# A decoder layer with 32 experts: expert outputs added into one array by accumulating scatters, and two-part matmuls in the narrow visits

## The chip, the cores and the metric

The kernel runs on one core of a Trainium2 chip. The core has TensorE (PE, with its weight loads shown apart as PEld), VectorE (DVE), ScalarE (ACT), GpSimd (POOL) and SyncE (SP, which here only issues DMAs). The metric is the device time of the whole program in microseconds (us).

## The reference

A layer norm, a combined input projection, a causal pooling mixer beside sparse attention (each query attends to the 256 keys that an indexer selects), an output projection, a residual with a layer norm (its result is called h1 here), and then a mixture of experts with a last residual and layer norm. What the change touches is the mixture of experts and what follows it:

```python
top_logit, top_e = lax.top_k(logits, TOP_K)          # 4 of 32 experts for each of 2048 tokens
gates = jax.nn.softmax(top_logit, axis=-1)
xs = xf[tok]                                         # 8192 rows of 1024, sorted by expert
hu = lax.ragged_dot(xs, w_gate_up, group_sizes) + b_gate_up[e_sorted]   # 1024 -> 2048
gate = jnp.minimum(hu[:, :D_FF], 7.0);  up = jnp.clip(hu[:, D_FF:], -7.0, 7.0)
act = (up + 1.0) * gate * jax.nn.sigmoid(1.702 * gate)
y = lax.ragged_dot(act, w_down, group_sizes) + b_down[e_sorted]         # 1024 -> 1024
out = jnp.zeros_like(xf).at[tok].add(y * g_sorted[:, None])
h = layer_norm(2 ** 0.25 * h + out, ln2_g, ln2_b)
```

All arrays are float32. With the reference's own inputs the experts get, sorted, 356 338 337 329 309 300 300 300 297 285 277 272 269 268 267 261 258 252 249 246 239 235 227 227 209 207 202 200 193 185 167 131 rows.

## The kernel before

Five stages follow each other, each a block with a barrier at its end: projection (to about 640 us of the span), attention with router (to 1840), a short placing stage (to 1854), the experts (to 4387) and the combination (to 4529).

**The experts stage** goes over "visits". A visit is one expert with up to 384 of its rows; here there are 32, widest first. An expert's row count is rounded up to a class of `WIDTHS` (L64: 384, 368, ... 240 in steps of 16), and PE runs one unrolled loop per class (`visit`, L2059; `loop`, L2083). Every engine goes through the visits in its own fixed program order:

- SP streams 12 MB of weights in six chunks of 2 MB through three buffers `w_raw` (`chunk`, L1878). Chunks 0 to 3 hold gate and up weights, 4 and 5 the down weights. It also stores the third row tile of the visit before (`store_third`, L1900), in 12 small DMAs.
- ACT rounds each chunk to `w_hi` (`high`, L2180), DVE computes the rest `w_lo = w_raw - w_hi` (`low`, L2102). The rows `x` are split the same way into `x_hi` and `x_lo`. Each product is then three fast-format matmuls: hi*hi, hi*lo, lo*hi (`passes`, L1995).
- Up part (`up_chunk`, L2007): for each of 8 blocks j of 128 hidden columns, 24 matmuls make the gate sum and 24 the up sum, into the two halves of PSUM pair `gu[j % 2]`. So 8 * 48 = 384 matmuls per visit, each as wide as the class. DVE adds bias, clips, and multiplies (`out_of_psum`, `activate`, L2114 to L2132), ACT does the sigmoid and rounds to `a_hi`, POOL makes `a_lo` and a copy `a_rest` (L1972). DVE and ACT work at 384 columns in every class.
- Down part (L2065): six tiles n of 128 rows x 512 columns in `yp[n % 2]`: n = 0, 1, 2 for the first half of the columns, 3, 4, 5 for the second. The third row tile (n = 2, 5) is a packed short form below 321 rows and nothing at 256 rows or fewer. Between them PE turns the rows of the next visit (`e_tr`). ACT copies each tile to `y_rows` (three buffers, `store`, L2204) and writes the first two row tiles of each half into `y_dram`, an array with one row for each (visit, place).
- POOL fetches the list of the next visit's tokens and gathers their rows of h1 (`gather`, L1953), at the head of the body, once the current visit's `x` has been turned.

**The combination stage** (L2257) gathers for each of 16 tiles of 128 tokens the 4 rows of `y_dram` that belong to each token (64 gathers of 128 rows of 4 KB, L2327), sums them with the gates by matmul (L2369) on top of a matmul for the gated `b_down` (L2362), and DVE and POOL do residual and layer norm (L2397 to L2415). Before that, positions of all picks are worked out on DVE and sent through DRAM to get them in pick order (`pos_list`, `gate_list`). `y_dram` is cleared for the spare visits by 12 DMAs in the projection stage (L615).

**The lists.** In the attention stage's routing DVE works out each token's place in its experts' lists (`weigh`, L1305), and POOL scatters the token numbers there (L1186), one DMA per pick.

## Time and profile before

| | us |
|---|---|
| median of 3 runs | 4528.32 (4526.23 to 4531.88) |
| span of the profiled execution | 4529.3 |
| experts stage, first up matmul to the end of the last visit | 1880.5 to 4381 |
| combination stage | 4387 to 4529.3 |

The page gives the profiled execution no other time of its own than its span, which is 1.0 us above the median of the runs. A busy share is the time in which an engine had at least one instruction running; PE's matmuls overlap in the records (each is shown longer than the distance to the next one), so the pace is read from the length of a stretch divided by its matmuls. Whole stages can be bound by different engines, so shares are read per stretch.

### The profile page before, as it was taken

Reading aid. Unit: us, or ns where it says so; the run is one execution under the profiler, and the core shown is the slowest. Engines: PE = TensorE matmul, PEld = TensorE weight load, DVE = VectorE, ACT = ScalarE, POOL = GpSimd, SP = SyncE. Lnnn points to the kernel's source line nnn. Section 1 sums busy time; section 2 is a strip of 40 time slices with the busy share of each in tenths; the row PEclk is TensorE's granted clock in tenths of the full one; section 3 lists DMA queues with packets and bytes.
Section 4 is the critical chain, followed back from the end, with each engine's and each line's share of the span. In section 5 each row is a group of like instructions: output and inputs, shape, how many; then the busy total and the mean of one; then the engine's idle time right before and its main releaser. Section 6 shows DMA issues by size and latency. Waiting matters only on the chain. (4 is left out here: it accounts for less than half of the span.)

```text
span 4529.3 us, 70549 instructions
## 1 busy us (share of the span) xinstructions
PE 4289.9 (95%) x24356; PEld 3153.5 (70%) x24356; DVE 3076.1 (68%) x4861; ACT 1817.6 (40%) x2677; POOL 1010.1 (22%) x1152
## 2 busy tenths in 40 slices
PE   8999988999999998699999999999999999999987
PEld 4444434444444454599989889899999999999961
DVE  2587867878888873555556556666676777777768
ACT  1222223443434433233434444444445555555530
POOL 1111101221111122211112212222222222222235
PEclk9999989999999999799999999999999999999986
DMA  6443330120110010544555456474657667667668
GB/s 194 126 122 92 87 101 16 30 27 21 18 23 16 14 27 19 148 158 148 174 168 190 155 183 220 162 250 161 237 197 239 208 230 241 219 234 237 212 214 362
DMA packets 534140, 665.72 MB, mean 147 GB/s; under 512 B 64416, under 2 KB 402592, under 8 KB 533952
## 3 DMA queue, kind: packets, MB, share of 16 engines
q1 hardware_dynamic: 419664, 501.02, 34.7%
q10 hardware_dynamic: 87744, 77.15, 5.4%
q0 software_dynamic: 26576, 85.56, 5.0%
q8 instruction: 87, 1.43, 0.1%
q14 instruction: 69, 0.57, 0.0%
HBM read 543.61 MB, written 120.03 MB: 147 GB/s over the span
## 5 line engine op out<-in xcount | busy, mean ns | idle before, releaser
L2000 PE MATMUL gu<-x_hi,w_hi 128*128 128x240 f32 (+8 forms) x4096 | 1196.5, 292 | 4.1 <-issue 4.1
L2003 PE MATMUL gu<-x_lo,w_hi 128*128 128x240 f32 (+8 forms) x4096 | 1195.5, 292 | 0.5 <-issue 0.5
L2004 PE MATMUL gu<-x_hi,w_lo 128*128 128x240 f32 (+8 forms) x4096 | 1194.1, 292 | 0.0
L2106 DVE TENSOR_TENSOR w_lo<-w_raw,w_hi 128x2048 fp32r<-128x2048 f32 x386 | 874.6, 2287 | 414.1 <-ACT w_hi L2190 386.2
L2190 ACT ACTIVATE w_hi<-w_raw 128x2048 fp32r<-128x2048 f32 x386 | 726.8, 1908 | 207.4 <-PE gu L2004 132.0
L2000 PEld LDWEIGHTS gu<-x_hi,w_hi 128*128 128x128 f32 x4096 | 774.7, 189 | 4.5 <-issue 4.3
L2003 PEld LDWEIGHTS gu<-x_lo,w_hi 128*128 128x128 f32 x4096 | 773.3, 189 | 1.1 <-issue 0.9
L2004 PEld LDWEIGHTS gu<-x_hi,w_lo 128*128 128x128 f32 x4096 | 773.8, 189 | 0.0
L1972 POOL TENSOR_TENSOR a_lo<-up,a_hi 128x384 fp32r<-128x384 f32 x256 | 396.6, 1549 | 1177.8 <-ACT a_hi L2202 1177.8
L570 PE MATMUL proj_acc<-w_in_sb,hT 128*128 128x512 f32 (+1 forms) x1280 | 499.0, 537 | 0.7 <-ACT hT L586 0.7
L2000 PE MATMUL yp<-w_hi,a_hi 128*128 128x512 f32 x1088 | 445.6, 410 | 2.3
L2003 PE MATMUL yp<-w_lo,a_hi 128*128 128x512 f32 x1088 | 431.4, 397 | 0.0
L2004 PE MATMUL yp<-w_hi,a_lo 128*128 128x512 f32 x1088 | 431.1, 396 | 0.0
L570 PEld LDWEIGHTS proj_acc<-w_in_sb,hT 128*128 128x128 f32 x1280 | 213.9, 192 | 221.4 <-issue 215.7
L2117 DVE TENSOR_SCALAR gate<-gu,b_gu 128x384 f32<-128x384 f32 x256 | 157.3, 614 | 279.0 <-PE gu L2004 278.8
L2202 ACT ACTIVATE a_hi<-up 128x384 fp32r<-128x384 f32 x256 | 134.5, 525 | 384.5 <-DVE up L2132 384.5
L2198 ACT ACTIVATE sig<-gate 128x384 f32<-128x384 f32 x256 | 132.7, 518 | 313.3 <-DVE gate L2117 312.5
L1212 DVE TENSOR_SCALAR_CACHE_REDUCE reach<-scores_odd,small 128x1792 bf16<-128x1792 f32 (+3 forms) x128 | 248.7, 1943 | 9.5 <-issue 1.1
L2000 PEld LDWEIGHTS yp<-w_hi,a_hi 128*128 128x128 f32 x1088 | 205.2, 189 | 64.9 <-POOL a_rest L1973 11.9
L1388 PE MATMUL qk<-kT,q_blk 128*128 128x512 f32 (+3 forms) x480 | 225.2, 552 | 19.4 <-ACT probs L1556 7.7
L2209 ACT ACTIVATE y_rows<-yp 128x512 f32<-128x512 f32 x192 | 113.9, 593 | 322.8 <-PE yp L2004 272.5
L1245 DVE TENSOR_REDUCE small<-qk 128x1 f32<-128x256 f32 (+15 forms) x96 | 123.6, 1288 | 172.3 <-PE qk L1390 170.9
(316 smaller groups left out, 5878.6 us busy)
## 6 DMA issues: line engine op xcount, KB each, us to landing
w_raw<-w_gate_up SPq DMA_DIRECT2D x258, 1024.0 KB, 7.6
w_raw<-w_down SPq DMA_DIRECT2D x128, 1024.0 KB, 8.1
y_dram<-y_rows ACTq DMA_DIRECT2D x128, 256.0 KB, 2.6
y_dram<-zeros ACTq DMA_DIRECT2D x12, 2688.0 KB, 15.5
h_blk<-h_dram SPq DMA_DIRECT2D x32, 512.0 KB, 8.7
qi_dram<-qi_stage ACTq DMA_DIRECT2D x16, 640.0 KB, 3.2
x_in<-x SPq DMA_DIRECT2D x16, 512.0 KB, 6.1
w_in_sb<-w_in SPq DMA_DIRECT2D x4, 2048.0 KB, 14.2
```

Source lines behind the costliest of these rows:

```text
L570: mm = nc.tensor.matmul(acc[:, (5 * t + n) % ACCS, 0:width], hT[:, t % 2, k], w_in[:, k, c0:c0 + width], start=(k == 0), stop=(k == KD - 1))
L1212: nc.vector.tensor_scalar(out, row, limit, 0.0, ALU.is_ge, ALU.add, accum_out=n_reach)
L1388: nc.tensor.matmul(out[:, at:at + width], q[:, k % 2, i], S["kT"][:, i // REP, at:at + width], start=True, stop=False)
L1972: nc.gpsimd.tensor_tensor(a_lo[:, j], up[:, j % 2], a_hi[:, j].bitcast(F32), ALU.subtract)
L2000: op = nc.tensor.matmul(out, s_hi_, m_hi, start=(n == 0), stop=False)
L2003: nc.tensor.matmul(out, s_hi_, m_lo, start=False, stop=False)
L2004: op = nc.tensor.matmul(out, s_lo_, m_hi, start=False, stop=(n == len(pairs) - 1))
L2106: nc.vector.tensor_tensor(w_lo[:, c % 2, cols], raw[:, c % 3, cols], w_hi[:, c % 2, cols].bitcast(F32), ALU.subtract).then_inc(s_lo, 1)
L2117: nc.vector.tensor_scalar(g, gu[:, j % 2, 0, 0:ROWS], S["b_gu"][:, j, bass.ds(e, 1)], LIMIT, ALU.add, ALU.min).then_inc(s_gm, 1)
L2190: nc.scalar.activation(w_hi[:, c % 2, cols], raw[:, c % 3, cols], ACT.Copy).then_inc(s_hi, 1)
L2198: nc.scalar.activation(sig[:, j % 2], gate[:, j % 2], ACT.Sigmoid, scale=SWI_ALPHA).then_inc(s_sig, 1)
L2202: nc.scalar.activation(a_hi[:, j], up[:, j % 2], ACT.Copy).then_inc(s_ah, 1)
```

## The change

1. **Sums in DRAM.** `y_dram` goes. A new array `sums` (2048 tokens and 512 dump rows) starts as a copy of h1, and each visit's output tiles, scaled by gate / 2^0.25 in ACT's copy out of PSUM, are added into it by indirect DMAs with an add, issued by POOL: 7 per visit (four of 128 x 2 KB, one of 128 x 2 KB and two of 128 x 1 KB for the third row tile). A list entry is now the pair (token, gate); unused places point to dump rows. SP's 12 store DMAs per visit and ACT's 4 go; SP gets 5 small loads (`load_third`) per visit. Adds of one visit may start only when all of the visit before have landed (`hold_places`), since two visits can hold the same token.
2. **Combination.** It reads `sums` tile by tile, adds the gated `b_down` (matmul), and normalises. ACT takes the statistics. The 64 gathers, the pick-order relay and the clearing of `y_dram` go. A factor 2^0.25 drops out in the layer norm.
3. **Classes.** 384, 368, 352, 320, 304, 288, 272, 256, 240, 208: 336 and everything else between is rounded up, 208 is new.
4. **Narrow visits** (256 rows or fewer): per weight block one matmul of `w_hi` against `x_hi` and `x_lo` side by side into two sums in the PSUM half, and one of `w_lo` against `x_hi`: 2 instead of 3 matmuls, the same columns. ACT copies the second sums with the bias to SBUF, DVE adds first and second sum for gate and up in one instruction. ACT and DVE work at 256 columns there. DVE and ACT get separate loops for wide and narrow visits.

```diff
-WIDTHS = tuple(range(ROWS, 2 * P - 17, -GRAIN))
+WIDTHS = (384, 368, 352, 320, 304, 288, 272, 256, 240, 208)
...
+                for name in ("h1", "sums"):
+                    sp.dma_start(D_[name][SEQ:, :].rearrange("(m p) n -> p m n", p=P),
+                                 res[:].unsqueeze(1).broadcast_to([P, 1 + ROWS // P, D])).then_inc(s_clear, 16)
...
-                    sp.dma_start(D_["h1"][b * P:(b + 1) * P, :], h1[:]).then_inc(s_h1st, 16)
+                    for name in ("h1", "sums"):
+                        sp.dma_start(D_[name][b * P:(b + 1) * P, :], h1[:]).then_inc(s_h1st, 16)
...
-                    nc.vector.tensor_copy(at_i[:], at_f).then_inc(s_at, 1)
+                    nc.vector.tensor_copy(at_i[:], at_f)
+                    nc.vector.tensor_copy(entry[:, :, 0], token[:, b:b + 1].broadcast_to([P, TOP_E]))
...
+                    nc.vector.tensor_scalar(entry[:, :, 1].bitcast(F32), e_gate, e_inv, 1.0 / ALPHA_RES,
+                                            ALU.mult, ALU.mult).then_inc(s_at, 1)
...
+                def load_third(v):
+                    at = look_up(sp, v, 1, MOST)
+                    rest, few = (look_up(sp, v, what, 1) for what in (2, 3))
+                    if not first(v):
+                        sp.wait_ge(s_hold, v)
+                    for i in range(4):
+                        row = at + 2 * P + i * FEW - rest * ((i - i % 2) * FEW) - few * (i % 2 * FEW)
+                        sp.dma_start(third[i * FEW:(i + 1) * FEW], D_["lists"][bass.ds(row, FEW), :]
+                                     ).then_inc(s_third, 16)
+                    sp.dma_start(spot[:], A["spots"][bass.ds(rest + few, 1)].rearrange("o p j n -> (o p) j n")
+                                 ).then_inc(s_third, 16)
...
                         if first(v) and c == 0:
                             sp.wait_ge(s_who, 16)
+                            load_third(0)
...
+                        if c == 5:
+                            load_third(v + 1)
                         chunk(v, c, e)
...
+                def hold_places(v):
+                    if not first(v):
+                        pool.wait_ge(s_yst[0], 32 * v)
+                        pool.wait_ge(s_yst[1], 32 * v)
+                        pool.wait_ge(s_yst[2], 32 * v)
+                        pool.wait_ge(s_yst[3], 16 * v)
+                    pool.wait_ge(s_third, 80 * v + 80)
...
+                def scatter(v, n):
+                    pool.wait_ge(s_y, 6 * v + n + 3)
+                    nc.gpsimd.tensor_tensor(idle[:, n:n + 1], zero[:, 0:1], zero[:, 0:1], ALU.add)
...
+                    for rows, at, part in parts:
+                        nc.gpsimd.indirect_dma_start(rows, bass.IndirectOffsetOnAxis(ap=at, axis=0), part, None,
+                                                     compute_op=ALU.add).then_inc(s_yst[3 if n == 5 else n % 3], 16)
...
                 def body(v):
+                    list_rows(v + 1)
                     gather(v + 1)
+                    if not first(v):
+                        scatter(v - 1, 5)
                     for j in range(J):
+                        if j == 2:
+                            hold_places(v)
+                        elif j == 3:
+                            hold_gates(v)
                         pool.wait_ge(s_ah, 8 * v + j + 1)
...
+                    for n in range(5):
+                        scatter(v, n)
...
+                def two_sums(bank, width, triples):
+                    out = bank.rearrange("p (s n) -> p s n", s=2)[:, :, 0:width]
+                    for n, (w_high, w_rest, moving) in enumerate(triples):
+                        nc.tensor.matmul(out, w_high, moving, start=(n == 0), stop=False)
+                        op = nc.tensor.matmul(out[:, 0], w_rest, moving[:, 0], start=False, stop=(n == len(triples) - 1))
+                    return op
...
+                    if parted:
+                        g, u = g[:, 0:2 * P], u[:, 0:2 * P]
+                        both = gate_up[:, j % 2, :, 0:2 * P]
+                        dve.wait_ge(s_sig, 24 * v + 3 * j + 2)
+                        nc.vector.tensor_tensor(both, gu[:, j % 2, :, 0:2 * P], both, ALU.add).then_inc(s_gu, 1)
+                        dve.drain()
+                        nc.vector.tensor_scalar(g, g, LIMIT, None, ALU.min).then_inc(s_gm, 1)
+                        nc.vector.tensor_scalar(u, u, LIMIT, -LIMIT, ALU.min, ALU.max)
+                        dve.drain()
+                        nc.vector.scalar_tensor_tensor(u, u, 1.0, g, ALU.add, ALU.mult)
+                        return
...
+                def second_sums(v, j, e):
+                    act.wait_ge(s_g1, 16 * v + 2 * j + 1)
+                    nc.scalar.activation(gate[:, j % 2, 0:2 * P], gu[:, j % 2, 0, 2 * P:], ACT.Identity,
+                                         bias=b_gate).then_inc(s_sig, 1)
+                    act.wait_ge(s_g1, 16 * v + 2 * j + 2)
+                    act.wait_ge(s_al, 8 * v + max(j - 1, 0))
+                    nc.scalar.activation(up[:, j % 2, 0:2 * P], gu[:, j % 2, 1, 2 * P:], ACT.Identity,
+                                         bias=b_up).then_inc(s_sig, 1)
...
+                        if slot < 2:
+                            act.wait_ge(s_yst[slot], 32 * v + 16 * (n // 3))
...
+                    nc.scalar.activation(y[:, slot], yp[:, n % 2], ACT.Copy, scale=gate_now[:, slot:slot + 1]
+                                         ).then_inc(s_y, 1)
...
                     for c in range(4):
                         high(v, c + 1, 0)
                         if c:
-                            sigmoid(v, 2 * c - 1)
+                            sigmoid(v, 2 * c - 1, parted)
                         high(v, c + 1, 1)
                         if c:
-                            high_act(v, 2 * c - 1)
+                            high_act(v, 2 * c - 1, parted)
...
+                        if parted:
+                            second_sums(v, 2 * c, e)
+                        sigmoid(v, 2 * c, parted)
+                        if parted:
+                            second_sums(v, 2 * c + 1, e)
+                        high_act(v, 2 * c, parted)
...
+                def add_bias(t):
+                    row = total[:, t % AHEAD]
+                    dve.wait_ge(s_in[t % AHEAD], 16 * (t // AHEAD + 1))
+                    dve.wait_ge(s_bias, t + 1)
+                    nc.vector.tensor_tensor(row, row, acc[:, t % SUMS], ALU.add).then_inc(s_tot, 1)
+
+                def finish(t):
+                    row = total[:, t % AHEAD]
+                    dve.wait_ge(s_square, t + 1)
+                    nc.vector.scalar_tensor_tensor(row, row, column(t, 1), gain[:], ALU.add, ALU.mult)
+                    dve.drain()
+                    dve.wait_ge(s_rstd, t + 1)
+                    nc.vector.scalar_tensor_tensor(row, row, column(t, 4), bias[:], ALU.mult, ALU.add
+                                                   ).then_inc(s_out, 1)
...
+                def spread(t):
+                    act.wait_ge(s_tot, t + 1)
+                    nc.scalar.activation(scratch[:, 0], row, ACT.Copy, accum_out=column(t, 0)).then_inc(s_mean, 1)
+                    act.wait_ge(s_mean, 2 * t + 1)
+                    nc.scalar.activation(column(t, 1), column(t, 0), ACT.Copy, scale=-1.0 / D).then_inc(s_mean, 1)
+                    act.wait_ge(s_mean, 2 * t + 2)
+                    nc.scalar.activation(scratch[:, 1], row, ACT.Square, bias=column(t, 1), accum_out=column(t, 2)
+                                         ).then_inc(s_square, 1)
```

## Rows read from the trace of the kernel before

**Rows 1.** The page, part 1: span, and PE's busy time, share, instructions.
```profile
span 4529.3 us, 70549 instructions
PE 4289.9 (95%) x24356; PEld 3153.5 (70%) x24356; DVE 3076.1 (68%) x4861; ACT 1817.6 (40%) x2677; POOL 1010.1 (22%) x1152
```
**Rows 2.** Windows: a stretch, its length, engines' busy (instructions), clock, DMA share, GB/s.
```profile
2083.60:2145.90 62.30, 62.30 (x385) 62.27 (x384) 36.03 (x43) 22.39 (x23) 13.58 (x16) 1.00 0.39 129
2182.30:2241.20 58.90, 58.90 (x385) 58.86 (x384) 36.03 (x43) 22.39 (x23) 12.63 (x14) 1.00 0.39 131
3413.10:3459.30 46.20, 46.20 (x388) 46.20 (x387) 35.68 (x43) 22.98 (x24) 14.17 (x16) 1.00 0.62 214
3899.50:3943.10 43.60, 43.60 (x388) 43.60 (x387) 35.69 (x43) 22.84 (x24) 13.73 (x15) 1.00 0.66 226
3943.10:3968.30 25.20, 25.06 (x119) 20.09 (x117) 15.44 (x17) 13.97 (x19) 4.25 (x7) 1.00 0.75 234
4387.00:4529.30 142.30, 99.90 (x336) 25.89 (x336) 104.76 (x131) 2.34 (x4) 88.12 (x81) 0.62 0.91 363
```
**Rows 3.** Groups by form, PE, experts stage: count, then busy us, mean ns.
```profile
L2000 PE MATMUL gu<-x_hi,w_hi 128*128 128x240 f32 x1536 | 424.6, 276 | 0.0
```
**Rows 4.** Timeline of PE inside a 240 visit: start, length, instructions.
```profile
3955.51 0.60 PE L1991 MATMUL e_tr<-ident,x_rows 128*128 128x128 f32 x4
3955.94 0.31 PE L2056 MATMUL yp<-so_far,ident 128*128 128x32 f32 x2
```
**Rows 5.** Groups of DVE and ACT, whole span: busy us, mean ns, idle before.
```profile
L2106 DVE TENSOR_TENSOR w_lo<-w_raw,w_hi 128x2048 fp32r<-128x2048 f32 x386 | 874.6, 2287 | 414.1 <-ACT w_hi L2190 386.2 <-issue 27.9
L2190 ACT ACTIVATE w_hi<-w_raw 128x2048 fp32r<-128x2048 f32 x386 | 726.8, 1908 | 207.4 <-PE gu L2004 132.0 <-issue 28.2 <-DMA w_raw<-w_gate_up 24.9
L2132 DVE TENSOR_TENSOR up<-up,sig 128x384 f32<-128x384 f32 x256 | 143.0, 558 | 21.4
L2198 ACT ACTIVATE sig<-gate 128x384 f32<-128x384 f32 x256 | 132.7, 518 | 313.3 <-DVE gate L2117 312.5
```
**Rows 6.** Timelines of ACT and POOL in the visit that starts at 3899.5.
```profile
3904.81 0.58 ACT L2209 ACTIVATE y_rows<-yp 128x512 f32<-128x512 f32 x1
3950.83 0.57 ACT L2209 ACTIVATE y_rows<-yp 128x512 f32<-128x512 f32 x1
3962.42 0.60 ACT L2209 ACTIVATE y_rows<-yp 128x512 f32<-128x512 f32 x1 [0.54 <-PE yp L2004]
3963.33 0.80 POOL L1958 DMA_DIRECT2D who<-lists_dram  x1 [14.74 <-PE e_tr L1991]
3968.74 0.96 POOL L1964 DMA_INDIRECT x_rows<-h_dram,who_now  x1 [0.30 <-issue]
```
**Rows 7.** DMA issues: count, KB each, median us from issue to landing.
```profile
x_rows<-h_dram,who_now POOLq DMA_INDIRECT x99, 7.5
rows<-y_dram,pos_by_pick POOLq DMA_INDIRECT x64, 18.4
```
**Rows 8.** Groups of the combination stage: busy us, mean ns, idle before.
```profile
L2397 DVE SCALAR_TENSOR_TENSOR total<-h_blk,c_acc 128x1024 f32<-128x1024 f32 x16 | 19.5, 1220 | 27.2 <-PE c_acc L2369 26.8 <-DMA out<-total 0.4
L2362 PE MATMUL c_acc<-b_down_sb,by_expertT 32*128 32x512 f32 x64 | 45.5, 845 | 0.0
```
**Rows 9.** Timelines around the experts stage's two ends and the span's end.
```profile
1853.51 0.21 POOL L1703 TENSOR_SCALAR_AFFINE_SELECT mine<-mine 128x32 f32<-128x32 f32 x1 [6.52 <-issue]
1858.90 17.76 SPq L1888 DMA_DIRECT2D w_raw<-w_gate_up  x6
4386.59 0.20 ACT L2254 ACTIVATE y_rows<-y_rows 128x1 f32<-128x1 f32 x1 [3.64 <-DMA y_dram<-y_rows]
4525.00 1.23 DVE L2415 TENSOR_TENSOR total<-total,bias 128x1024 f32<-128x1024 f32 x1
```
**Rows 10.** Windows of the projection stage, one with clearing DMAs, one without.
```profile
200.00:300.00 100.00, 95.53 (x333) 44.98 (x332) 80.52 (x248) 23.85 (x60) 16.22 (x10) 1.00 0.46 134
500.00:600.00 100.00, 95.47 (x350) 40.61 (x348) 74.11 (x178) 29.39 (x70) 11.45 (x8) 1.00 0.09 32
```

More of the change, by code:

```diff
@@ L63 @@
 GRAIN = 16
-WIDTHS = tuple(range(ROWS, 2 * P - 17, -GRAIN))
+WIDTHS = (384, 368, 352, 320, 304, 288, 272, 256, 240, 208)
+KINDS = tuple((ROWS - width) // GRAIN for width in WIDTHS)
+LAST_KIND = tuple(kind - 1 for kind in KINDS[1:]) + KINDS[-1:]
+ONE_SUM = sum(width > 2 * P for width in WIDTHS)
+PEELED = 2
 REST = 64
@@ L90, in project_stage @@
     GAPS = 16
-    CLEARS = 12
-    SHARE = (MAX_VISITS - EXPERTS) * ROWS // CLEARS
-    SHARE_N = next(n for n in range(1, SHARE + 1) if SHARE % n == 0 and SHARE // n <= P)
-    assert SHARE * CLEARS == (MAX_VISITS - EXPERTS) * ROWS
     CHUNKS = [(n * BANK, min(BANK, IN_W - n * BANK)) for n in range(5)]
@@ L1966, in gather @@
                         ).then_inc(s_x, 16)
+                def hold_places(v):
[5 more added lines that the diff above has]
+                    pool.wait_ge(s_third, 80 * v + 80)
+                    nc.gpsimd.tensor_tensor(scaled[:], spot[:, :, 0], third[:, 0:1].broadcast_to([P, 3]), ALU.mult)
+                    for h in range(2):
+                        nc.gpsimd.tensor_scalar(at_main[:, :, h], held[:, 0:2, 0], 2.0, float(h), ALU.mult, ALU.add)
@@ L2175, in _, with high @@
                     low_x(0, k)
-                over_visits(dve, body)
+                more = dve.value_load(S["more"][0:1, 0:1], min_val=EXPERTS - 1, max_val=MAX_VISITS - 1)
+                one_sum = dve.value_load(S["ends"][0:1, ONE_SUM - 1:ONE_SUM], min_val=PEELED, max_val=MAX_VISITS - 1)
+                body(0, False)
+                with dve.Fori(1, one_sum) as v:
+                    body(v, False)
+                with dve.Fori(one_sum, more + 1) as v:
+                    body(v, True)
+                weigh_experts()
             @block.scalar
             def _(act):
-                def high(v, c, half):
+                def high(v, c, half, after=None):
                     n = 12 * v + 2 * c + half
@@ L2248, in _ @@
                     high_x(0, k)
-                n = over_visits(act, body)
+                more = act.value_load(S["more"][0:1, 0:1], min_val=EXPERTS - 1, max_val=MAX_VISITS - 1)
+                one_sum = act.value_load(S["ends"][0:1, ONE_SUM - 1:ONE_SUM], min_val=PEELED, max_val=MAX_VISITS - 1)
+                body(0, False)
+                with act.Fori(1, one_sum) as v:
+                    body(v, False)
+                with act.Fori(one_sum - 1, more) as before:
+                    body(before + 1, True, before)
+                n = more + 1
                 store(n - 1, 5)
-                act.wait_ge(s_yst[0], 32 * n)
-                act.wait_ge(s_yst[1], 32 * n)
-                act.wait_ge(s_yst[2], 192 * n)
-                nc.scalar.activation(y[:, 0, 0:1], y[:, 0, 0:1], ACT.Copy)
 def combine_stage(nc, A, S, D_):
@@ L2316, in _ @@
                     sp.wait_ge(s_out, t + 1)
-                    sp.dma_start(out_dram[t * P:(t + 1) * P, :], total[:, t % OUTS]).then_inc(s_st[t % OUTS], 16)
-                for n in range(OUTS):
-                    sp.wait_ge(s_st[n], 16 * len(range(n, TILES, OUTS)))
+                    sp.dma_start(out_dram[t * P:(t + 1) * P, :], total[:, t % AHEAD]).then_inc(s_st[t % AHEAD], 16)
+                    if t >= 1 and t - 1 + AHEAD < TILES:
+                        load(t - 1 + AHEAD)
+                for n in range(AHEAD):
+                    sp.wait_ge(s_st[n], 16 * len(range(n, TILES, AHEAD)))
@@ L2345, in _ @@
+                    nc.gpsimd.tensor_scalar(column(t, 3), column(t, 2), 1.0 / D, EPS / ALPHA_RES ** 2,
+                                            ALU.mult, ALU.add)
+                    pool.drain()
+                    nc.gpsimd.tensor_tensor(column(t, 4), column(t, 3), minus_half[:], ALU.pow).then_inc(s_rstd, 1)
             @block.tensor
             def _(pe):
-                pe.wait_ge(s_by, 1)
                 for g in range(TILES // 4):
@@ L2374, in _ @@
+                    op.then_inc(s_bias, 1)
             @block.vector
             def _(dve):
[L2376 to L2381 removed]
@@ L2407, in finish @@
-                def finish(t):
-                    slot = t % OUTS
-                    dve.wait_ge(s_rstd, t + 1)
-                    nc.vector.tensor_scalar(total[:, slot], total[:, slot], small[:, slot, 12:13], small[:, slot, 15:16],
-                                            ALU.subtract, ALU.mult)
-                    dve.drain()
-                    nc.vector.tensor_tensor(total[:, slot], total[:, slot], gain[:], ALU.mult)
-                    dve.drain()
-                    nc.vector.tensor_tensor(total[:, slot], total[:, slot], bias[:], ALU.add).then_inc(s_out, 1)
```

437 lines of the change are left out of this document (195 added, 242 removed).

## The prediction

> **What bounds the kernel now.** I read the page first: PE is busy for 95% of the span [rows 1]. That is an average, so the second view is the windows, one stretch at a time. In the experts stage each up part is full of matmuls: in the window of a 240 visit's up part PE is busy for all of it, weight loads too, and DVE for 35.7 of 43.6 us; in the down part PE is busy for 25.06 of 25.20 us [rows 2]. So over 1880 to 4381 PE alone sets the time, and DMAs, DVE, ACT and POOL lie beside it. The combination is different: 142.3 us, clock 0.62, DMA share 0.91 [rows 2]. There the DMA of the gathered rows is the bound, and its median landing is 18.4 us [rows 7].
>
> **PE's pace.** An up part is 384 matmuls. 46.20 / 384 = 120.3 ns at width 256, 43.60 / 384 = 113.5 ns at 240 [rows 2]. The difference is 6.7 ns for 16 columns, so 0.417 ns a column (the granted clock is 1.00, its 2.4 GHz level) and a fixed 13.5 ns for each matmul. The count of 240-wide matmuls, 1536 on one of three lines at 128 a visit, is 12 visits [rows 3], as the experts' row counts say; 3 more are at 256.
>
> **Part 1, two-part matmuls and the class 208.** For each of the 128 weight blocks three matmuls become two, with the same columns: one fixed part of 13.5 ns goes, 128 * 13.5 = 1.7 us a visit. From the row counts, 3 visits are at 256, 5 stay at 240, and 7 go to 208. At 208 a block costs 416 + 208 = 624 columns, 260 ns, and 27 ns fixed: 128 * 287 = 36.7 us against 43.6, 6.9 us less. Gross: 8 * 1.7 + 7 * 6.9 = 61.9 us. No row shows a moving operand in two pieces. Bounds: at worst the two-part matmul costs like two matmuls (the 13.5 ns stay: nothing for eight visits, and for the seven 128 * 3 * (208 columns and 13.5 ns) = 38.5 us, 5.1 less each, 36 us in all); at best a second 13.5 ns goes with it (another 1.7 us a visit, 26 us). I take the sum by instruction, as the pace of every row here is fixed cost plus columns.
>
> Four turns with their loads are 0.43 us apart from the next matmul, 108 ns each, though 128 columns would be 53 + 13.5 ns [rows 4]: a weight load of 128 columns has a pace of its own. At 208 the short matmul (100 ns) is shorter than that by 8 ns, at worst 128 * 8 ns = 1.1 us a visit, 7 in all. I keep it in the range only. The Trainium skill (TensorE: Matmul & The Clock Gate, LDWEIGHTS) gives a load as its columns over 1.2, an estimate of 107 ns; the trace's 108 ns agrees. By that rule the 208 gain would be 7 us smaller.
>
> **Does the chain behind PE keep up in these visits?** Durations by a straight line through two shapes [rows 5]: ACT (0.518 at 384, 1.908 at 2048) 0.41 us at 256; DVE tensor_tensor (0.558, 2.287) 0.43 at 256 and 0.69 at 512; a clip at 256 taken as 0.28. Each j now needs 2 more ACT copies. One chunk is two j. In program order the loop is: ACT second sum of the odd j (0.41), rounding of a (0.41), first half of the next weight chunk (1.9), DVE low half (2.3), product with the sigmoid (0.43), low half (2.3), joined sum (0.7), clip (0.3), ACT sigmoid (0.45), second sum of the gate (0.45): with hand-overs about 9.8 us. PE needs 10.5 us a chunk at 240 and 11.1 at 256, so nothing is lost. At 208 PE needs 9.2, so the lead is eaten at 0.6 us a chunk: I lay the visit out so and find PE waiting 0.6 us for PSUM in the last chunk and 1.4 us for the last `a_lo` in the first down tile. 2.0 * 7 = 14 us. For the other eight 0.2 each, 2 us. Net of part 1: 61.9 - 16 = 46 us. If DVE or ACT instructions cost nothing more, it would be 62; if the loop ran twice as late, 32.
>
> **Part 2, classes.** One expert (329 rows) goes from 336 to 352: 62.3 - 58.9 = 3.4 us more [rows 2].
>
> **Part 3, the combination.** Before: from 4387.0 to the end, 142.3 us. After: no gathers. A tile moves 0.5 MB in and 0.5 out, 16.8 MB in all; at the 363 GB/s of the row that is 46 us, no longer the bound. DVE has three passes of 1024 columns, each about 1.22 [rows 8], with gaps 3.9 us a tile. PE has the bias matmul, 4 records of 0.85 mean [rows 8], 3.4 us a tile or 3.7 at the low clock: beside DVE. ACT's two passes (by the line 1.05 each) and their small parts are about 3 us: beside DVE. So 16 * 3.9 = 62 us. In front stand 16 turns and the first bias matmul at the low clock, and the first load, about 8 us; behind, the last store: the last vector instruction ended at 4526.2, 3.1 us before the end [rows 9]. 8 + 62 + 3 = 73, with 1 us for the last tile's statistics 74. Gain 142.3 - 74 = 68 us. From both sides: DMA-bound, 46 + 11 = 57 (gain 85); DVE and ACT serialised on the column dependencies, 5 us a tile, 91 (gain 51).
>
> **Part 4, the adding scatters.** POOL gets 7 indirect DMAs at about 1.0 us issue (the gather's row [rows 6]) plus 0.3, six tiny instructions and some small ones: 11 us a visit, in the idle time of an engine that is busy 13.7 + 4.3 us of 68.8 [rows 2]. What counts is what is queued behind a wait:
> - The adds of visit v's tile 5 are issued only after the gather at the head of v+1. In the visit from 3899.5 ACT stores tile 5 at 3904.8. The list fetch stood at 3963.3, before the visit ended [rows 6]; it now stands behind the scatter of tile 4, 7 us later, the gathers after it, so the scatter of tile 5 goes out about 13 us into the visit. The rows of x arrive at about 20 us; they are needed at 37 or later. Then `hold_places` waits at j = 2 until the add has landed, and `a_lo` of j = 2, ready at 19 to 22 us, stands behind it; DVE and ACT want `up[0]` back at 23 to 26 us. A landing of up to 10 us costs nothing at 240 and 1 us or less at 208.
> - ACT's copy of tile 3 waits for the add of tile 0. The copies are at 3950.8 and 3962.4 [rows 6]; scatter issued at about 3953, so 9.6 us are free and 3.3 more until PE feels it. Before, this was a plain store.
> - SP's chunk 5 now stands behind `hold_gates` and 5 loads. It moves from about 12 to 24 us into the visit, lands about 10 us later and is needed at 41 or later. In return 12 store DMAs leave that queue.
> The cost of the add is not in this trace. The nearest rows: the gather of 128 rows of 4 KB lands in 7.5 us (median), that of the saturated combination in 18.4 [rows 7]. An adding row of 2 KB reads twice and writes once, so its bytes are near the first. I take 8 us, so no stall; at 18.4 us see the rival. The Trainium skill (Collectives: The Full Stack, on ReduceScatter against AllGather) says that an adding transfer reads two sources and so runs at half the rate. No run here shows it yet; for 1.57 MB a visit it would be the traffic of 3.1 MB, still beside PE by the DMA share of 0.66 to 0.75 in rows 2.
>
> End of the stage: before, ACT waited 3.6 us for its last store [rows 9]. Now POOL issues two more scatters behind it and the add takes longer: 4.5 us more.
>
> **Part 5, the rest.** Start: the placing stage ended with POOL's selects after 6.5 us of waiting [rows 9]; without them DVE ends it, 2.3 us earlier. SP issued its first weights at 1858.9; five small loads with their registers now come first, taken as 3.5 us. Net 1 us more. Clearing: PE is busy 95.5 us in a window with the clearing DMAs and in one without [rows 10]: nothing gained. Attention: two small DVE instructions per tile beside a busy PE, and a second store on SP: 1 us, bounds -1 and 8 (16 * 0.5).
>
> **The sum.** 4529.3 - 46 + 3.4 - 68 + 4.5 + 1 + 1 = 4425.2. The profiled execution is 1.0 above the median of the runs, so I say 4425.
>
> **Rivals.**
> - A, slower: *the adds land late*, as the gathers of the combination do (18.4 us). For: those rows are adds' kin (indirect, one row per descriptor), each add touches DRAM twice, and they share the engines with 0.7 of weight traffic. Against: the x gathers under that traffic land in 7.5. Price: tile 3's copy waits until 3953 + 18.4 = 3971.4 against 3965.7 free, 5.7 us; `hold_places` releases `a_lo` at 32.4 us and PE waits about 2.6. 8.3 us * 32 visits = 266: 4691. It decides from landings of about 13 us; it makes the whole slower when a visit loses more than 104 / 32 = 3.3 us, at a landing of some 16 us.
> - B, *the adds are a partial cost*: landings of 12 to 15 us, 0.5 to 2.5 us a visit; at 1.5, 48 us: 4473.
> - C, *the narrow matmuls don't do what they say*: the two-part stream paces like two matmuls, and DVE and ACT hold PE. Only 208's columns, 36 - 16 = 20 us instead of 46, remain: 4451; with the loop limiting all fifteen, nothing: 4471.
> - D, *no net change*: A's mechanism at 3.3 us, 4529.
>
> **How the numbers follow.** Forecast 0.62, A 0.11, B 0.14, C 0.12, D 0.01. The likeliest one's own range is 4400 to 4450 (combination 51 to 85, part 1 32 to 62). The range takes in B and C and some of the high clock of the combination: 4398 to 4492; outside stay A, D and the ends, 0.2. A measurement of this kernel tells 0.2%, 9 us, from no change. Slower by more: A, 0.11 in all. Same: 0.02. Faster: 0.87.
>
> **What would show it.** Visits of 208 at 61 to 64 us, of 240 at 67.0 against 68.8, distance of a pair of matmuls 327 ns at 240; combination 70 to 78 us with DVE busy almost throughout; wide visits unchanged to 0.3 us. Landing of `sums` adds below 12 us. It is wrong if PE idles before tile 5 or the next up part for ACT's `y_rows` behind a DMA on `sums`, or if `a_lo` waits for POOL's small instructions at j = 2.

## The result, and the profile after

| | before | after |
|---|---|---|
| median of 4 runs, us | 4527.43 (4526.23 to 4531.88) | 4566.92 (4563.55 to 4570.03) |
| ratio after / before | | 1.0085, interval 1.0070 to 1.0099 |
| span of the profiled execution | 4529.3 | 4562.0 |
| first up matmul of the experts | 1880.5 | 1875.6 |
| experts stage | 2500.5 | 2605.0 |
| combination, from its first instruction | 142.3 | 71.2 |

Predicted was 4425, with 0.87 on faster. It is slower by 0.85%, outside the range of 4398 to 4492. The combination came out as forecast; the experts stage, where 42.6 us were to be won, lost 104.5.

The page's span and part 1 for the changed kernel [rows 1]:

```profile
span 4562.0 us, 67203 instructions
PE 4233.6 (93%) x22180; PEld 3096.5 (68%) x22180; DVE 2998.7 (66%) x4813; ACT 1920.4 (42%) x2997; POOL 1606.5 (35%) x1743
```

PE's instructions fall by 2176 and its busy time by 56 us, and the program is still longer: PE idles more. The windows say where: up part and down part of a 240 visit, an up part at 208, one at 272, and the combination [rows 2].

```profile
3744.80:3794.20 49.40, 44.11 (x259) 39.82 (x258) 33.25 (x43) 26.55 (x38) 24.00 (x28) 0.97 0.64 204
3794.20:3820.00 25.80, 24.98 (x119) 20.13 (x117) 15.43 (x17) 14.39 (x20) 14.77 (x13) 1.00 0.78 224
4042.90:4089.30 46.40, 40.09 (x259) 39.51 (x258) 32.39 (x42) 26.14 (x38) 22.97 (x28) 0.93 0.64 205
3198.00:3251.20 53.20, 50.39 (x388) 50.17 (x387) 36.54 (x43) 22.94 (x24) 29.01 (x29) 0.97 0.67 223
4490.80:4562.00 71.20, 55.11 (x80) 21.55 (x80) 58.04 (x48) 43.62 (x84) 15.53 (x33) 0.52 0.68 253
```

An up part at 240 was 43.6 us with PE busy in all of it; now it is 49.4 with 44.1 busy. The down part is nearly what it was (25.2, now 25.8). So PE stands for 5.3 us once in this visit, in the up part, and no engine is full there. The waits of the twelve visits at 240 and 208, 3594 to 4480, name a chain (engine, line, what it waited for, us in total, times, longest):

```profile
DVE gate_up L2169 <- ACT gate_up L2275: 119.0, 40, 7.3
ACT gate_up L2275 <- POOL a_rest L1999: 98.5, 12, 8.2
PE gu L2046 <- DVE gate_up L2169: 70.8, 12, 6.3
```

Twelve waits of PE in twelve visits: PE waits for DVE to empty PSUM, DVE for ACT's second sum, ACT for POOL's `a_rest`. The three visits at 256 show the same wait of PE, 12.7 us in all. The four in the visit that starts at 3744.8, each on its engine's timeline (start, length):

```profile
3769.34 0.80 POOL L1999 COPY a_rest<-gate_up 128x64 f32<-128x64 f32 x1
3770.32 0.47 ACT L2275 ACTIVATE gate_up<-gu,b_gu 128x256 f32<-128x256 f32 x1 [8.20 <-POOL a_rest L1999]
3770.83 0.69 DVE L2169 TENSOR_TENSOR gate_up<-gu,gate_up 128x512 f32<-128x512 f32 x1 [7.32 <-ACT gate_up L2275]
3771.58 0.77 PE L2046 MATMUL gu<-x_both,w_hi 128*128 128x480 f32 x1 [5.29 <-DVE gate_up L2169]
```

ACT was idle from about 3762.1, 17.3 us into the visit. It wanted the slot `up[0]` for j = 2, and POOL gave it back only with the `a_rest` of j = 0, at 3770.1. POOL's own timeline shows why (scatter of tile 4, held list, list fetch, names, first gather, scatter of tile 5, `a_lo` of j = 0, `hold_places`) [rows 6]:

```profile
3745.98 1.56 POOL L1984 DMA_INDIRECT sums_dram<-y_rows,at_main  x1
3746.98 0.76 POOL L1936 COPY who_held<-who 128x6 int32<-128x6 int32 x1
3753.01 0.86 POOL L1940 DMA_DIRECT2D who<-lists_dram  x1 [5.26 <-issue]
3759.39 1.38 POOL L1945 TENSOR_TENSOR who_now<-who,zero 128x3 int32<-128x3 int32 x1 [5.53 <-DMA who<-lists_dram]
3761.67 2.77 POOL L1948 DMA_INDIRECT x_rows<-h_dram,who_now  x1 [0.90 <-issue]
...
3767.32 1.61 POOL L1984 DMA_INDIRECT sums_dram<-y_rows,at_third  x1 [0.17 <-issue]
3768.39 1.56 POOL L1998 TENSOR_TENSOR a_lo<-gate_up,a_hi 128x384 fp32r<-128x384 f32 x1
...
3773.40 0.20 POOL L1960 TENSOR_TENSOR scaled<-spot,third 128x3 int32<-128x3 int32 x1 [2.15 <-DMA sums_dram<-y_rows,at_third]
```

`a_lo` of j = 0 starts 23.6 us into the visit. Two entries fill the time. Between the held copy and the list fetch stand 5.26 us marked "issue": POOL waits for nothing that another engine does. It is the `pool.drain()` at L1937, behind an indirect DMA. The record also tells what this drain waits for. The scatter issued at 3745.98 lands 5.86 us later, at 3751.84, and the list fetch goes out 1.17 us behind the landing. In the visit from 3198.0 the scatter issued at 3199.15 lands 7.26 us later, at 3206.41, and the fetch again goes out 1.16 us behind. The landings of these two scatters, and the second fetch:

```profile
sums_dram<-y_rows,at_main POOLq DMA_INDIRECT x1, 5.9
sums_dram<-y_rows,at_main POOLq DMA_INDIRECT x1, 7.3
3207.57 0.85 POOL L1940 DMA_DIRECT2D who<-lists_dram  x1 [4.69 <-issue]
```

In all 31 visits with such a scatter the fetch follows the landing by 1.16 to 1.17 us, while the landings themselves run from 5.0 to 8.3 us. So the drain holds POOL until the added rows have landed. Then come 5.53 us for the list. `hold_places`, at which the prediction looked, stops POOL for another 2.15 us, when PE has already lost its time.

The wide visits show the same wait from 288 columns down, there on DVE (a visit at 272):

```profile
3224.67 0.62 DVE L2180 TENSOR_SCALAR gate_up<-gu,b_gu 128x384 f32<-128x384 f32 x1 [6.24 <-POOL a_rest L1999]
```

DMA issues from 1900 to 4480: count, median us to landing [rows 7]:

```profile
sums_dram<-y_rows,at_main POOLq DMA_INDIRECT x127, 7.3
sums_dram<-y_rows,at_third POOLq DMA_INDIRECT x95, 6.1
who<-lists_dram POOLq DMA_DIRECT2D x31, 3.0 KB, 5.2
```

### The profile page after: what moved, and what is told of

The parts are those of the page before. It is cut to its first block and busy times, and to the rows that moved or that the text cites. A ratio compares the mean times of both kernels' runs of the same rounds, so it can differ in the third digit from the quotient of the medians.

```text
span 4562.0 us, 67203 instructions
## 1 busy us (share of the span) xinstructions
PE 4233.6 (93%) x22180; PEld 3096.5 (68%) x22180; DVE 2998.7 (66%) x4813; ACT 1920.4 (42%) x2997; POOL 1606.5 (35%) x1743
## 5 line engine op out<-in xcount | busy, mean ns | idle before, releaser
L2261 ACT ACTIVATE w_hi<-w_raw 128x2048 fp32r<-128x2048 f32 x386 | 726.1, 1907 | 151.5 <-PE gu L2039 100.3
L2046 PE MATMUL gu<-x_both,w_hi 128*128 128x416 f32 (+2 forms) x1920 | 646.8, 390 | 83.5 <-DVE gate_up L2169 83.5
L2035 PE MATMUL gu<-x_both,w_hi 128*128 128x272 f32 (+5 forms) x2176 | 665.2, 306 | 27.2 <-DVE gate_up L2180 16.0
L2038 PE MATMUL gu<-x_both,w_hi 128*128 128x272 f32 (+5 forms) x2176 | 662.6, 304 | 0.0
L2039 PE MATMUL gu<-x_both,w_lo 128*128 128x272 f32 (+5 forms) x2176 | 661.4, 304 | 0.0
L1998 POOL TENSOR_TENSOR a_lo<-gate_up,a_hi 128x384 fp32r<-128x384 f32 x256 | 372.7, 1500 | 593.8 <-ACT a_hi L2287 590.9
L2047 PE MATMUL gu<-x_both,w_lo 128*128 128x208 f32 (+2 forms) x1920 | 527.4, 275 | 0.0
L2046 PEld LDWEIGHTS gu<-x_both,w_hi 128*128 128x128 f32 x1920 | 375.1, 195 | 126.9 <-DVE gate_up L2169 87.7
L2035 PEld LDWEIGHTS gu<-x_both,w_hi 128*128 128x128 f32 x2176 | 411.7, 189 | 29.7 <-DVE gate_up L2180 18.0
L2038 PEld LDWEIGHTS gu<-x_both,w_hi 128*128 128x128 f32 x2176 | 411.7, 189 | 0.2
L2039 PEld LDWEIGHTS gu<-x_both,w_lo 128*128 128x128 f32 x2176 | 411.5, 189 | 0.0
L2047 PEld LDWEIGHTS gu<-x_both,w_lo 128*128 128x128 f32 x1920 | 379.9, 198 | 0.0
L2301 ACT ACTIVATE y_rows<-yp,gate_now 128x512 f32<-128x512 f32 x192 | 131.0, 683 | 374.7 <-PE yp L2039 306.2
L2287 ACT ACTIVATE a_hi<-gate_up 128x384 fp32r<-128x384 f32 (+1 forms) x256 | 121.2, 474 | 324.1 <-DVE gate_up L2192 321.7
```

The lines of the kernel that those rows point to most:

```text
L1998: nc.gpsimd.tensor_tensor(a_lo[:, j], up[:, j % 2], a_hi[:, j].bitcast(F32), ALU.subtract)
L2035: op = nc.tensor.matmul(out, s_hi_, m_hi, start=(n == 0), stop=False)
L2038: nc.tensor.matmul(out, s_hi_, m_lo, start=False, stop=False)
L2039: op = nc.tensor.matmul(out, s_lo_, m_hi, start=False, stop=(n == len(pairs) - 1))
L2046: nc.tensor.matmul(out, w_high, moving, start=(n == 0), stop=False)
L2047: op = nc.tensor.matmul(out[:, 0], w_rest, moving[:, 0], start=False, stop=(n == len(triples) - 1))
```

## The experiments

Theories. **Q** (queue at the head): a visit is late because POOL, in program order, does drain, list fetch, names, gathers and scatter before the first `a_lo`. **L**: the adding itself is the cost, by its landing or its traffic. **N**: the two-part matmuls with ACT's second sums and DVE's joined sum are the cost. All ratios are to the kernel before, run beside them on their chip: 4546.9 us beside e1 to e4, 4546.67 beside e5 to e8. The table above is from another chip, where the kernel before took 4527.43.

**e1, the list fetched early.** POOL has the same instructions and one tiny one more per visit; their order changes. The held copy, its drain and the list fetch of visit v+2 stand at j = 5, the names ahead of the scatters.

```diff
 def body(v):
-    list_rows(v + 1)          # held copy, drain, list fetch
-    gather(v + 1)             # wait for the list, names, drain, 3 gathers
+    gather(v + 1)             # 3 gathers
     if not first(v): scatter(v - 1, 5)
     for j in range(J):
+        elif j == 5: list_rows(v + 2)
         ...
+    name_rows(v + 2)          # wait for the list, names, drain
     for n in range(5): scatter(v, n)
```

> The changed kernel with GpSimd's order altered: the copy of the list and the fetch of the next list stand at j = 5 of the visit before, and the row numbers are made ready ahead of the scatters, so that no drain stands behind an adding scatter; the three gathers go out first thing in the visit. The adds themselves are unchanged. Theory Q (GpSimd's queue: the 5.6 us drain behind the scatter of tile 4 puts gathers, the last scatter and a_lo of j = 0 to 2 some 10 us late): TensorE's stalls in the up part (6.5 us a visit at 240, 7.8 at 208, 1.8 to 4.5 at 272) fall to 1 us or less; 32 visits together lose 100 us less, so about 4460 to 4475. Theory L (the adds land too late, 6.7 us median): the wait on the landed add stays, less than 30 us are gained, above 4530. Theory N (the narrow visits' longer chain over ScalarE and VectorE is the bound): the 272 visits recover, the narrow ones keep 4 us or more of stall: 4520 to 4540.

Measured: 4450.59 us (4448.98 to 4452.04), ratio 0.9786 (0.9769 to 0.9802), faster than both kernels, and some 10 us better than Q had let expect. On POOL's timeline of the 240 visit from 3711.7, the end of the visit before and then the head:

```profile
3712.84 1.55 POOL L1989 DMA_INDIRECT sums_dram<-y_rows,at_main  x1 [0.15 <-issue]
...
3714.78 1.01 POOL L1953 DMA_INDIRECT x_rows<-h_dram,who_now  x1 [0.16 <-issue]
...
3720.50 1.62 POOL L1989 DMA_INDIRECT sums_dram<-y_rows,at_third  x1 [0.16 <-issue]
3723.48 1.02 POOL L2004 TENSOR_TENSOR a_lo<-gate_up,a_hi 128x384 fp32r<-128x384 f32 x1 [1.36 <-ACT a_hi L2297]
...
3746.82 0.87 POOL L1938 DMA_DIRECT2D who<-lists_dram  x1 [0.77 <-issue]
```

Tile 5 is scattered 8.8 us into the visit, `a_lo` waits for ACT and not ACT for it, and the same drain, away from the scatters, takes 0.77 us instead of 5.26. The up parts at 240, 208 and 272 (in the order of the windows):

```profile
3711.70:3754.00 42.30, 42.30 (x259) 38.71 (x259) 33.35 (x43) 26.39 (x38) 24.36 (x28) 1.00 0.73 237
3980.50:4019.00 38.50, 38.50 (x259) 38.24 (x259) 32.81 (x41) 25.85 (x37) 24.36 (x28) 1.00 0.76 241
3207.70:3256.40 48.70, 48.70 (x387) 48.70 (x386) 35.94 (x43) 23.05 (x24) 25.29 (x29) 1.00 0.72 244
```

PE is busy in all of them, the adds and the narrow code still in place. The experts stage is 2467.3 us, 137.7 less than in the changed kernel: about 58 of it in the seven visits at 208, 35 in the five at 240, 20 in the three at 256, 20 in the six at 272. Q holds. L and N fall as the main cause; L's landing counts only through the drain that waits for it.

**e2, plain scatters.** The rows overwrite those in `sums` and are not added: the sum over experts is left out. Traffic that reads `sums` goes.

```diff
-indirect_dma_start(rows, IndirectOffsetOnAxis(ap=at, axis=0), part, None, compute_op=ALU.add)
+indirect_dma_start(rows, IndirectOffsetOnAxis(ap=at, axis=0), part, None)
```

> The changed kernel with the add left out of the scatters: they write the rows instead of adding them (what several experts give to one token is then not summed). The same DMAs, the same order, the same waits. Theory L: landing falls from 6.7 to about 3 us and the stalls go, 4480 or less. Theory Q: the drain stays at about 5 us; only the wait on the landed add (47 us in all on this trace's hold step) shrinks: 4530 to 4560. Theory N: no change within 5 us.

Measured: 4484.77 us (4478.70 to 4495.58), ratio 0.9865 (0.9847 to 0.9882). So it removes most of the loss, though the order of the queue is untouched; it lies between the ranges of L and Q. It looks like L, but POOL's timeline says more (240 visit from 3726.5):

```profile
3727.68 0.98 POOL L1984 DMA_INDIRECT sums_dram<-y_rows,at_main  x1
3728.67 0.19 POOL L1936 COPY who_held<-who 128x6 int32<-128x6 int32 x1
3732.77 0.82 POOL L1940 DMA_DIRECT2D who<-lists_dram  x1 [3.91 <-issue]
3735.19 0.19 POOL L1945 TENSOR_TENSOR who_now<-who,zero 128x3 int32<-128x3 int32 x1 [1.61 <-DMA who<-lists_dram]
```

The scatter's issue is 0.98 us instead of 1.56, the drain behind it 3.91 instead of 5.26, the list 1.61 instead of 5.53 us of waiting. Tile 5 goes out 13.8 us into the visit (3740.30), and the 240 visits take 68.65 to 68.77 us but for the first (72.0). By e1 the same adds cost nothing once drain and list stand elsewhere.

The drain is shorter because a plain scatter lands sooner; here too the fetch goes out 1.15 us behind the landing, in all 31 visits. The list's wait has another reason than the add, since behind the drain the scatter has landed. Its landing goes with the weight traffic that it meets. Windows over the first 2 to 3 us of four list loads, which landed in 6.3 us (changed kernel, 240), 2.3 us (changed kernel, a visit at 352, also behind an adding scatter), 2.3 us (e2, 240) and 5.6 us (e1, at j = 5, with no scatter near it); the last but one number is the DMA share:

```profile
3753.00:3756.00 3.00, 3.00 (x20) 2.72 (x19) 1.36 (x5) 0.97 (x3) 0.86 (x1) 1.00 0.66 221
2082.70:2085.00 2.30, 2.30 (x17) 2.30 (x16) 2.03 (x1) 2.30 (x3) 0.85 (x1) 1.00 0.04 1
3732.80:3735.00 2.20, 2.20 (x15) 2.01 (x14) 2.11 (x3) 0.00 (x0) 0.79 (x1) 1.00 0.04 1
3746.90:3749.90 3.00, 3.00 (x19) 2.74 (x19) 2.84 (x3) 2.10 (x3) 0.85 (x2) 1.00 1.06 394
```

So at 240 e2's list load goes out early enough to fall into a gap between two weight chunks. Where it does not, e2 keeps much of the stall: at 272 the drain takes 5.66 us and the list 5.56, and a visit is 78.9 us, against 77.8 in e1 and 79.5 to 82.3 in the changed kernel.

**e3, three matmuls per block everywhere.** The two-part matmuls, the second sums and the joined sum go, DVE and ACT work at 384 columns; classes, adds and POOL's order stay.

```diff
-if width <= 2 * P:  op = two_sums(...)
+if False:           op = two_sums(...)
```

> The changed kernel with part 4 of the change undone: all visits with three matmuls per block and VectorE and ScalarE at 384 columns; the classes, 208 among them, stay. Theory N: the narrow visits lose their stalls, the result is 30 us or more faster than the changed kernel. Theory Q: the stalls stay, since VectorE's write of up waits for the same a_lo; matmuls pace at 100 ns at 208, so the result lies within 15 us of the changed kernel, 4555 to 4580.

Measured: 4592.32 us (4587.38 to 4596.29), ratio 1.0102 (1.0085 to 1.0118). The visits at 240 and at 208 both take about 75 us, and the up part is 6.8 us longer than without the stall (e8 below). PE stands for 4.2 of them; the granted clock of the up part is 0.93. The stall doesn't come from the narrow code. N falls. With the stall there, the narrow code gains next to nothing: 1.0102 without it, 1.0091 with it (e5).

**e4, the narrow part alone.** The kernel before with the new classes and narrow visits, without adds and with its own combination.

```diff
-WIDTHS = tuple(range(ROWS, 2 * P - 17, -GRAIN))
+WIDTHS = (384, 368, 352, 320, 304, 288, 272, 256, 240, 208)
...
+if width <= 2 * P:  op = two_sums(...)
```

> The kernel before with parts 3 and 4 of the change alone (classes and the two-part matmuls with VectorE's joined sum); outputs stored and combined as before, no adding scatters. By the pitches of the changed trace (331 ns a pair at 240, 352 at 256, 301 at 208) the up parts are 42.4, 45.1 and 38.5 us: 5 * 1.2 + 3 * 1.1 + 7 * 5.1 = 45 us less, 3.4 more for the class 336, 0 to 14 for the chain: 4486 to 4500. Theory N: the chain of ScalarE and VectorE stalls TensorE here too, 4 us or more a narrow visit: 4530 or more.

Measured: 4515.46 us (4509.49 to 4528.57), ratio 0.9937 (0.9918 to 0.9956), 31 us less. Visits: 70.6 us at 256, 68.03 at 240, 65.4 at 208, and no stall. That is 15 us or more short of what was expected: the up part at 208 is 38.6 us as forecast, but the down part is 26.8 where before had 25.2. The change's second half works by itself.

**e5, the changed kernel again**, beside e6 to e8, so that neither, one or both halves of the head can be compared on one chip.

> The changed kernel as it is, to have it on the same chip as the next three: ratio to before 1.0085, TensorE's up parts 49.4 us at 240, with 6.5 us of stall, and 72.8 us a visit at 208.

Measured: 4585.37 us (4584.00 to 4594.38), ratio 1.0091 (1.0074 to 1.0107); the first chip's 1.0085 stands.

**e6 and e7, each half of the head alone.** e6 is e1 with one more drain at the head; e7 is e1 with the list fetch, its wait and the names back at the head, the held copy and its drain left at j = 5.

```diff
 def body(v):                            # e6
+    pool.drain()
     gather(v + 1)
```
```diff
 def body(v):                            # e7
+    list_rows(v + 1)          # list fetch only; held copy and drain at j == 5
+    ...                       # wait for the list, names, drain
     gather(v + 1)
```

> The version of e1 with one drain of GpSimd added as the first thing in each visit, right behind the scatter of tile 4; nothing else. If the drain alone is the loss (theory Q in its narrow form), it takes 4 to 6 us there, and most of the stall comes back: 60 us or more slower than e1. If it takes the drain and the in-line fetch of the list together, GpSimd runs about 5 us later than in e1, the adds of tile 5 go out at 14 us into the visit instead of 9, and TensorE stalls 0 to 1 us a visit: 0 to 25 us slower than e1, ratio to before 0.979 to 0.984.

> The changed kernel with the copy of the list and its drain moved to j = 5 of the visit before, but the fetch of the next list, its landing (5.5 us) and the row numbers at the head, behind the scatter of tile 4, as in the change. If only the long drain mattered, it comes out as e1. If drain and fetch add up, some 5 of the 13 us of delay go: TensorE's stall falls from 6.5 to 1 to 3 us a visit at 240, ratio to before 0.985 to 0.997.

Measured: e6 4461.69 us (4454.94 to 4467.43), ratio 0.9816 (0.9800 to 0.9833); e7 4464.54 us (4461.81 to 4468.93), ratio 0.9821 (0.9805 to 0.9838). Each alone costs about 0.3% over e1, both together 3%; for e7 0.985 to 0.997 had been expected. On POOL's timeline, e6 and then e7:

```profile
3701.33 1.55 POOL L1989 DMA_INDIRECT sums_dram<-y_rows,at_main  x1 [0.16 <-issue]
3707.61 0.19 POOL L1951 TENSOR_TENSOR idle<-zero 128x1 int32<-128x1 int32 x1 [4.73 <-issue]
```
```profile
3711.41 0.92 POOL L1938 DMA_DIRECT2D who<-lists_dram  x1
3716.08 0.28 POOL L1947 TENSOR_TENSOR who_now<-who,zero 128x3 int32<-128x3 int32 x1 [3.75 <-DMA who<-lists_dram]
```

Both costs are there, 4.73 and 3.75 us on POOL, and hardly reach PE. Medians over the 240 visits, in us into the visit, and the lengths of visits:

| | scatter of tile 5 | `a_lo` of j = 0 | `a_lo` of j = 2 | visit at 240 | at 208 |
|---|---|---|---|---|---|
| e1 | 8.8 | 11.8 | 22.4 | 68.03 | 64.70 |
| e6 | 12.6 | 13.7 | 23.3 | 68.03 | 65.3 or 68.0 |
| e7 | 13.1 | 14.3 | 23.7 | 68.44 | 66.41 |
| e2 | 13.8 | 16.8 | 23.9 | 68.75 | 66.42 |
| after | 22.4 | 23.5 | 28.9 | 75.06 | 72.79 |

The first `a_lo` may be late to about 14 us for 0.4 us or nothing at 240, to 17 us for 0.7 us; from there to 23.5 it costs PE nearly its whole delay. 5 and 4 us fit into that slack one at a time and not together. At 208, where a j is shorter, the fetch alone costs 1.7 us, and the drain alone about 0.6 us in three visits and 3.3 in three others.

**e8, e1 without the narrow code.** e3's edit on e1.

> The version of e1 with three matmuls per block in all visits (part 4 undone, classes kept). No stalls, up parts 43.6 us at 240, 46.2 at 256 and, at the pitch of 112 ns that the run without part 4 had at 208, 43.0 us there: 5 * 1.3 + 3 * 1.2 + 7 * 4.5 = 42 us slower than e1, ratio to before 0.988. If the weight load does not set 208's pace but the columns do (100 ns), 38.5 us and 10 us slower than e1: 0.981.

Measured: 4488.16 us (4486.03 to 4489.68), ratio 0.9871 (0.9855 to 0.9888). So the narrow code is worth 4488.16 - 4450.59 = 37.6 us, once the queue is free. Its up parts at 240 and at 208:

```profile
3709.90:3752.80 42.90, 42.90 (x386) 42.90 (x386) 36.85 (x42) 22.30 (x23) 26.22 (x28) 1.00 0.70 231
3985.70:4028.70 43.00, 43.00 (x388) 43.00 (x387) 36.18 (x42) 22.29 (x23) 26.24 (x28) 1.00 0.71 232
```

Up to the first matmul of the next part they are 42.97 us at 240 and 42.95 at 208: with three matmuls a block, 32 columns fewer bring nothing.

## Why the prediction was wrong, step by step

**The step that failed** is part 4's first bullet: the list fetch "now stands behind the scatter of tile 4, 7 us later, the gathers after it, so the scatter of tile 5 goes out about 13 us into the visit", and from it "I take 8 us, so no stall". It goes out at 22.5 (3767.32 - 3744.8). The bullet counted the issues only: no drain and no landing at the head. By its 7 us the fetch would go out 2.0 us into the visit; it goes out at 8.2, 6.2 later, since the drain of the held copy now stands behind a scatter and waits for its landing (3746.98 to 3753.01). The prediction had that landing in its sum, at about the right 8 us, but let only tile 3's copy and `hold_places` wait for it. And the fetch, moved 13 us later, meets more traffic (DMA share 0.66 in its first 3 us, where before had 0.41) and lands later: from fetch to first gather 8.7 us, where before had 4.1 (3963.33 to 3967.43), 4.6 more. Before's own visits at 304 to 272, where the fetch met full weight traffic, already had landings of 5.8 to 5.9 us; the 4.1 came from a 240 visit. The rest, gathers to scatter, is 1.3 shorter than the bullet's 6.9. 6.2 + 4.6 - 1.3 = 9.5, the whole difference between 13 and 22.5. With it the "no stall" of the bullet became one of 5.3 us at 240, 6.3 at 208 and 1.5 to 2.8 at 272. A row of before showed such a wait, and the prediction itself quoted it: POOL's select after 6.52 us of "issue" behind the indirect scatters of the placing stage [rows 9]. It was read as waiting that would go, not as the price of a drain behind an indirect DMA.

A second error in the same bullet: it watched the `a_lo` of j = 2, behind `hold_places`, with `up[0]` wanted at 23 to 26 us. The limit that decided is one round earlier: `up[0]` after j = 0, which ACT wanted at 17.3 us.

**Rival A** had the right sign and an `a_lo` stuck in POOL's queue, but the wrong cause: its condition was landings of 13 us and more, and they are 7.3 and 6.1; the forecast 8 was near. Its stall was also in other places, at `hold_places` and at tile 3's copy. What it had right is that POOL would wait for a landing; it waits at the drain, and there 5 to 8 us are enough. **B** and **D** stood on the same landing. **C** falls as a cause of the loss: e4 and e8 show the narrow code at work, though below its forecast.

**PE's pace, part 1.** Visits at 240: forecast 67.0, in e1 68.03; at 208: 61 to 64, in e1 64.70. From the pitch of the up matmuls in e1, a pair at 240 takes 331 ns (forecast 327), at 256 352 (346.8), at 208 301 (287). So the sum lacked 14 ns a pair at 208, 14 ns * 128 = 1.8 us a visit, where the prediction's "a weight load of 128 columns has a pace of its own", kept "in the range only", gave 1.1 at worst. Whether this is that load is not shown. In e1's trace the short matmul at 208 takes 96 ns from its start to the next, where the sum had 100, and the two-part one 205, where it had 187; 4 to 5 ns a pair are also missing at 240 and 256, where the load was not expected to bind. With three matmuls a block there is such a limit: in e8, 42.95 us / 384 = 112 ns a matmul at 208. The Trainium skill (TensorE: Matmul & The Clock Gate, LDWEIGHTS) puts the load at an estimated 107 ns; e8's pace is 5 ns above. Of the forecast chain loss of 2.0 us at 208, the 0.6 in the up part did not come; the 1.4 for the last `a_lo` in the first down tile did, at 0.9 us on average in twelve visits of e1, its wait at PE being:

```profile
PE yp L2045 <- POOL a_rest L2005: 11.2, 12, 1.2
```

The down part is 1.0 us longer than before at 208 and 0.5 at 240. Net of part 1: forecast 46. The fifteen narrow visits of e1 are together about 34 us shorter than before's (4.1 each at 208, 0.7 at 240, 0.6 at 256), e8 against e1 gives 37.6 for the two-part matmuls, and e4 gives 31 with part 2's loss in it.

**Part 2.** 3.4 us forecast; the visit of 329 rows went from 95.3 to 100.26, 5.0 us, in this trace and to 97.1, 1.8 us, in e5's. The 352-wide visits now run at either of two paces, 97.1 or 100.3 us, where before both took 98.7; what sets the pace stays open.

**Part 3.** 74 us forecast, 71.2 measured. DVE sets the pace, as forecast: three passes of mean 1277, 1284 and 1214 ns a tile, one tile every 3.69 us where 3.9 was taken.

```profile
L2466 DVE SCALAR_TENSOR_TENSOR total<-total,small,bias 128x1024 f32<-128x1024 f32 x16 | 20.5, 1284 | 1.2
L2463 DVE SCALAR_TENSOR_TENSOR total<-total,small,gain 128x1024 f32<-128x1024 f32 x16 | 20.4, 1277 | 0.0
L2458 DVE TENSOR_TENSOR total<-total,c_acc 128x1024 f32<-128x1024 f32 x16 | 19.4, 1214 | 16.7 <-PE c_acc L2448 16.7
```

The end of the experts stage: forecast 4.5 us more, measured 4.3 (10.3 between the last matmul and the next stage, 6.0 before).

**Part 4's other bullets** hold: ACT's copies wait 12.0 us for adds in the twelve visits at 240 and 208, and PE waits 2.4 us in all for them (2.4 in e1 too), and chunk 5 of the weights ends none of PE's waits. In e1 PE waits for nothing in the narrow visits' up parts.

**Part 5.** SP's first weights now go out 8.9 us behind the stage's first instruction on POOL, where before it was 4.5 [rows 9]; forecast were 3.5 us more for the small loads, it is 4.4:

```profile
1845.51 0.10 POOL L2003 MEMSET zero<- 128x3 int32 x1 [5.29 <-POOLq L1687]
1851.44 2.17 SPq L1911 DMA_DIRECT2D third<-lists_dram  x4
1854.38 19.05 SPq L1894 DMA_DIRECT2D w_raw<-w_gate_up  x8
```

The placing stage is 2.3 us shorter, as forecast. What was before it, forecast at 1 us more, came out 6.6 us shorter; no run takes it apart, and the cause stays open.

**The sum.** e1's ratio times 4527.4 gives 4430 us; the forecast was 4425. By stages, e1's trace against that of before: experts 33.2 us less (forecast 42.6), combination 70.9 less (68); of e1's 96.3 us that leaves 7.8 lost elsewhere (6.5). So the sum was near what this change gives if POOL's queue has room, with part 1 some 12 us short. It was wrong by one queue, in which every instruction was there to be counted.

## What to carry to other kernels

When a step is moved onto a queue with indirect DMAs, write that engine's queue out with a price for every entry, drains, small fetches and their landings too, up to the first instruction that another engine waits for, and compare with when that one is wanted. A drain behind an indirect DMA is a wait for its landing, so price it as one. Take such a drain, and a small load that would meet full weight traffic, and put them in front of it, or into the middle of other work: here moving both turned 0.9% slower into 2.1% faster. Costs that meet one slack don't add: each half alone cost 0.3%, both 3%, so an experiment that removes one of two can hide or overstate either.
